# Two sets of weight buffers instead of three, with eight ring slots for row pairs and twelve for value rows

## The reference, cut to what matters

```python
def block(xb):                                    # 128 tokens; x is the normalised h
    q = einsum('td,de->te', xb, w_q)              # 8 heads x 2 halves x 128
    s = einsum('thpd,hpkd->thpk', q, keys)        # scores against 128 keys a half
    s_top, i_top = top_k(s, 16)
    cand = s_top[:, :, 0, :, None] + s_top[:, :, 1, None, :]
    best, sel = top_k(cand, 16)                   # 16 of 256 pairs of keys
    eidx = take_along_axis(cand_idx, sel)         # rows of 16384 experts
    gate = softmax(best)
    act = gelu(einsum('td,thkd->thk', xb, u_tab[eidx]))
    return einsum('thk,thkd->td', gate * act, v_tab[eidx])
y = rmsnorm(h + block(...), norm_final)
```

## Time and profile before

| | us |
|---|---|
| median of 3 runs | 2121.41 |
| lowest and highest | 2119.64, 2131.3 |
| profiled execution | 2125.79 |
| its span | 2123.7 |
| TensorE busy (matmul) | 1930.8, 91% |
| VectorE busy | 1360.7, 64% |
| ScalarE busy | 608.8, 29% |
| GpSimd busy | 634.1, 30% |
| first part of the stage | about 820 to 1503 |
| second part of the stage | about 1520 to 2116 |

### The profile page before, as it was taken

How to read it: one execution, slowest core, us unless ns; L and a number is a source line. 1 busy time by engine, 2 the same in 40 slices (tenths; PEclk the granted TensorE clock), 3 DMA queues, 4 the chain that set the end, 5 groups by cost and what they waited for, 6 DMA issues and landing times. The chain is left out here.

```text
span 2123.7 us, 29758 instructions
## 1 busy us (share of the span) xinstructions
PE 1930.8 (91%) x10912; PEld 1566.5 (74%) x10912; DVE 1360.7 (64%) x2860; ACT 608.8 (29%) x1217; POOL 634.1 (30%) x556
## 2 busy tenths in 40 slices
PE   5998889988996988989999999999899989999886
PEld 4997889977976988989999999989444333433332
DVE  3218274343346435479889888989677778776663
ACT  4223322252234424444444544444300000000000
POOL 0003021200000000312222222222477776776663
PEclk9999899998998999999999999999999999999999
DMA  3557158628614664799999999999899999999997
GB/s 114 195 198 228 34 165 268 224 75 268 214 59 146 227 234 145 289 341 385 374 369 391 379 383 363 370 363 378 314 412 411 395 410 411 398 400 415 408 412 289
DMA packets 230314, 629.25 MB, mean 296 GB/s; under 512 B 19714, under 2 KB 121157, under 8 KB 212376
## 3 DMA queue, kind: packets, MB, share of 16 engines
q0 software_dynamic: 74880, 377.52, 45.1%
q1 hardware_dynamic: 155296, 249.92, 34.5%
HBM read 584.36 MB, written 110.21 MB: 327 GB/s over the span
## 5 line engine op out<-in xcount | busy, mean ns | idle before, releaser
L2139 PE MATMUL ps<-ex_uv_row,ex_q_s 128*128 128x512 f32 (+1 forms) x1208 | 543.3, 601 | 62.4 <-DVE ex_q_s L2403 40.0
L2139 PEld LDWEIGHTS ps<-ex_uv_row,ex_q_s 128*128 128x128 f32 (+1 forms) x1208 | 217.3, 187 | 372.2 <-issue 355.8
L2068 POOL DMA_INDIRECT ex_uv_row<-value_rows,ex_eidx x384 | 404.5, 1053 | 187.5 <-issue 106.7
L589 PE MATMUL ps<-x_hi,ex_w_lo 128*128 128x384 f32 (+2 forms) x1296 | 426.3, 329 | 14.7 <-DVE ex_w_lo L1937 13.5
L590 PE MATMUL ps<-x_lo,ex_w_hi 128*128 128x384 f32 (+2 forms) x1296 | 424.4, 327 | 0.0
L591 PE MATMUL ps<-x_hi,ex_w_hi 128*128 128x384 f32 (+2 forms) x1296 | 424.2, 327 | 0.0
L2052 POOL DMA_INDIRECT ex_uv_row<-in_peer_uv,ex_eidx x128 | 147.3, 1151 | 470.3 <-DVE ex_fin L2390 464.7
L2390 DVE SCALAR_TENSOR_TENSOR ex_fin<-ex_uv_row,ret_tables,ex_fin 128x1024 f32<-128x1024 f32 x218 | 278.9, 1280 | 0.3
L589 PEld LDWEIGHTS ps<-x_hi,ex_w_lo 128*128 128x128 f32 x1296 | 245.1, 189 | 16.3 <-DVE ex_w_lo L1937 14.8
L591 PEld LDWEIGHTS ps<-x_hi,ex_w_hi 128*128 128x128 f32 x1296 | 245.5, 189 | 0.0
L590 PEld LDWEIGHTS ps<-x_lo,ex_w_hi 128*128 128x128 f32 x1296 | 245.3, 189 | 0.0
(11 more groups left out here) (415 smaller groups left out, 3417.7 us busy)
## 6 DMA issues: line engine op xcount, KB each, us to landing
value_rows<-in_peer_uv SPq DMA_DIRECT2D x64, 1024.0 KB
ex_w_raw<-in_peer_ut SPq DMA_DIRECT2D x128, 512.0 KB
value_rows<-ex_z_rows SPq DMA_DIRECT2D x128, 128.0 KB
first_raw<-in_w_in SPq DMA_DIRECT2D x8, 1024.0 KB, 7.6
ex_w_raw<-in_peer_wqt SPq DMA_DIRECT2D x16, 512.0 KB
value_rows<-ex_z_rows SPq DMA_DIRECT2D x128, 64.0 KB
dp_w_raw<-in_w_in SPq DMA_DIRECT2D x14, 512.0 KB
ex_uv_row<-value_rows,ex_eidx POOLq DMA_INDIRECT x384
```

Of the source, the lines that this page charges most:

```text
L589: pe.matmul(out, left(llo, c), right(rhi, c), start=(c == 0), stop=False)
L2068: pool.indirect_dma_start(value_slot(p)[0], None, k.value_rows, bass.IndirectOffsetOnAxis(ap=eidx[:, u, n % TOPK:n % TOPK + 1], axis=0), e ...
L2139: ins = pe.matmul(k.pv[j % 2][0:r, c, :], spread[:, on_tensor[p] % SPREADS, 0:r], v[:, c * 512:(c + 1) * 512], start=first, stop=last)
```

## The change

`DEEP` goes from 3 to 2, `RING` from 7 to 8 and `VALUES` from 10 to 12. With two sets, SyncE loads block i+2 in step i where it loaded i+3, after the low part of block i. ScalarE rounds block i+1 where it rounded i+2, after the same event. VectorE lowers block i+1 where it lowered i+2. The load and the rounding of block 2 ahead of the loop go away, as they are now part of it, and so does GpSimd's low part of block 4, which VectorE takes. The final gain uses the other buffer. The ring's memory grows from 56 to 64 KB a partition. As 136 pairs divide by 8, the value slots now begin at its start, and twelve fit.

```diff
--- before.py
+++ after.py
@@ -67,13 +67,13 @@
 HK = PH * TOPK
 NE = NK * NK
 PER_ROW = HK * NS // P
-RING = 7
-DEEP = 3
+RING = 8
+DEEP = 2
 AHEAD = 5
 BT = NP_TOK - P
 WROW = D + BT
 VALUE_SLOT = D + 2 * P
-VALUES = 10
+VALUES = 12
 ROWS_FROM = 6
 SPREADS = 6
 PARTS_AT = (1, 4, 7, 10)
@@ -1874,7 +1874,7 @@
         shift, tot = sb("shift", [P, UNITS + 1]), sb("tot", [P, UNITS + 1])
         eidx = sb("eidx", [P, UNITS + 1, TOPK], U32)
         eidx_s, gate_s = sb("eidx_s", [P, PER_ROW], U32), sb("gate_s", [P, PER_ROW])
-        x_rep, gain = sb("x_rep", [P, D])[:, :], w_raw[1][:, :, :].rearrange("p c n -> p (c n)")
+        x_rep, gain = sb("x_rep", [P, D])[:, :], w_raw[0][:, :, :].rearrange("p c n -> p (c n)")
         coef = k.ret[:, 0:SLOTS]
         fin, ms, unused = sb("fin", [P, 2, D]), sb("ms", [P, NT]), sb("unused", [P, 1])
         x_rest = flat(q)[:, 4 * D:8 * D].rearrange("p (t d) -> p t d", d=D)
@@ -1913,7 +1913,7 @@
 
         def by_dve(i):
 
-            return i not in (2, 3, 4)
+            return i not in (2, 3)
 
         def lowered(eng, i):
 
@@ -1994,7 +1994,6 @@
                 load(1)
                 for dst, src in h_out:
                     sp.dma_start(dst, src).then_inc(h_stored, 16)
-                load(2)
                 sp.wait_ge(h_stored, 32)
                 fetch(0)
                 fetch(1)
@@ -2069,7 +2068,7 @@
                                             bass.IndirectOffsetOnAxis(ap=eidx[:, u, n % TOPK:n % TOPK + 1], axis=0),
                                             element_offset=0 if n // HK == 1 else P).then_inc(value_loaded[b], 16)
 
-                for i in (2, 3, 4):
+                for i in (2, 3):
                     lower(pool, i)
                 for p in range(AHEAD):
                     gather_pair(p)
@@ -2275,7 +2274,6 @@
                 act.activation(q[:, 0:2, 0:P], k.pb[4][:, 0:2 * P].rearrange("p (n t) -> p n t", n=2),
                                ACT.Copy).then_inc(first_taken, 1)
                 upper_x(2)
-                upper(2)
                 upper_x(3)
                 upper_x(4)
                 act.wait_ge(cleared, 1)
@@ -2285,8 +2283,8 @@
                     elif i:
                         take(blocks[i - 1][1], 0)
                         take(blocks[i - 1][1], 1)
-                    if i and i + 2 < len(blocks):
-                        upper(i + 2)
+                    if i and i + 1 < len(blocks):
+                        upper(i + 1)
                     if row_at.get(i, 0) > 0:
                         row(row_at[i] - 1)
                     if i in weight_at:
@@ -2468,8 +2466,8 @@
                 retrieve(0)
                 for i in range(len(blocks)):
                     p = row_at.get(i, -1)
-                    if 5 <= i + 2 < len(blocks) and by_dve(i + 2):
-                        lower(dve, i + 2)
+                    if 4 <= i + 1 < len(blocks):
+                        lower(dve, i + 1)
                     if p >= 0:
                         dot(p)
                     if 1 < p <= HK + 1:
```

## The result

The changed kernel takes 2177.14 us (median of 4 runs, 2170.81 to 2180.03) beside 2126.36 for the kernel before (4 runs on the same chip, 2119.64 to 2132.22): a ratio of 1.022, 95% interval 1.0189 to 1.0251, so 2.2% slower. The forecast was 2183. Its mechanism, the turn of a weight buffer, is in the trace. How the sum came to 62 us holds less well, and that is what most experiments are about.

What follows compares the result with a forecast made beforehand. TensorE and the DMA engines were both taken as full beside the blocks, the DMA engines as binding the value part. Terms 25 + 30 + 6 + 8 - 2 - 5 = +62 us gave 2188, as a median 2183; range 2124 to 2262.

Steps and rivals of the forecast that it cites:

- The turn of a load: Experts' weight blocks: with two sets a buffer's turn, load to low part, exceeds two blocks' time; 0.2 us a block, +25 us.
- L: Time from a weight load's issue to its landing: 9.1 us read before, 6.5 assumed after; two sets hide 6.1.
- The retrieval on VectorE: Top-k parts beside the blocks make VectorE late with low parts and following loads: 0.75 us for each of 40, +30 us.
- The start: Opening of the experts stage: block 2's load waits for block 0's low part, amid eight gathers: +6 us (0 to +14).
- SyncE's lists: Two lists of small transfers issued between weight loads; with one set less, more of each delay is seen: +8 us.
- The ring slot: An eighth slot for pair gathers helps only in the last pairs, which have no blocks beside them: -2 us.
- The value slots: Twelve slots in the value part bring its DMA rate nearer its best slices: -5 us (-17 to 0).
- A: Two weight sets are enough, load time falling below 6.1 us: 2128 us, chance 0.13.
- B: Faster: no load late, lists and first burst hidden, value part at 412 GB/s: 2099 us, chance 0.10.
- C: The queue stays, load time remaining 9.1 us whatever the pace: +192 us on the blocks, 2320 us, chance 0.08.
- D: TensorE's pauses also drop its granted clock, once in each of nine units: +31 us on the forecast, 2214, chance 0.10.
- the marks set down: Signs expected in the trace: 16-block window, GB/s, TensorE's wait for low parts, load time, value part's length, clock mean.

Runs made afterwards that it cites:

- e7_a_dot: The changed kernel with the dots over 128 of 1024 columns, which relieves VectorE: 2173.59 us, ratio 1.0191.
- e4_b_raw2: The kernel before with only the loaded weights (w_raw) cut to two buffers: 2162.12 us, ratio 1.014.
- e1_raw3: The changed kernel with a third buffer for the loaded weights (w_raw) only: 2149.87 us, ratio 1.0086.
- e2_z3: The changed kernel with a third z_rows buffer only: 2176.9 us, ratio 1.0213.
- e3_raw3z3: The changed kernel with three w_raw and three z_rows buffers, two sets of rounded and low parts: 2130.39 us, ratio 1.0001.
- e10_r7v10: The changed kernel with seven ring slots and ten value slots: 2174.07 us, ratio 1.0211.
- e9_c_dot: e3_raw3z3 with the dots over 128 of 1024 columns: 2118.5 us, ratio 0.9962.
- e5_a_half: The changed kernel with pair gathers of half the size (only u, which stands in for v): 2121.42 us, ratio 0.9956.
- e6_b_half: The kernel before with pair gathers of half the size (only u, which stands in for v): 2103.44 us, ratio 0.9856.

## Why the prediction was right, and where its sum was not

**The turn of a load: the mechanism right, the size too low.** The prediction took L = 6.5 us between 4.0 and 9.1; measured 6.6 in the mean. That it came so near is luck: it was the middle of two values, and the 9.1 was read from two loads where the mean of the kernel before is 8.1. The load goes out ahead of the gather by 2.6 us (2.4 forecast), and half-size gathers lower L to 4.8, so it is shown that the gathers beside it make it long. Which of the two reasons that were given for a shorter L did it, the order or the slower pace, wasn't separated.

In the kernel before the turn wasn't what paced the loads, as SyncE's waits show, so that its 10.3 us of room with three sets is no limit there: one load in ten took over 10.3 us, and TensorE waited twice in the 110 blocks.

But (L + 2.31) / 2 with L = 6.5 gave 0.2 us a block and +25. The 110 blocks lost 42.8 us, 0.39 each. One mean L was put into a formula in which the loads over the limit count most; the early ones give nothing back beyond two sets. In the kernel after 75 of the 110 loads are above 6.1 us, by 90 us in all, and half of that, as a turn spans two blocks, is 45. That it comes so close is not to be relied on: in e7_a_dot the same sum gives 59 us, and its blocks lost 43.5. By the experiments the loads' third buffer is worth 30 us where all else has three (e4_b_raw2), 28 where z_rows stays at two (e1_raw3 against after), and 45 where z_rows has three (e2_z3 against e3_raw3z3: 0.0212 x 2127), of which 27 are in the 110 blocks and 7.5 in the opening, where block 2 is loaded earlier again.

The Trainium skill ("DMA: Bandwidth & Descriptors", on the anatomy of one DMA) would have a 512 KB load at an estimated 3.2 us; the page gives its figures for a transfer that GpSimd issues, and these loads are SyncE's. Not even the changed kernel, at 346 GB/s, comes near: 6.6 us. With gathers of half the size it is 4.8.

**The retrieval on VectorE: the addition failed.** It was to add 30 us to the turn. The waits that it named are there, 17.8 us in the 110 blocks, but e7_a_dot shows that relieving VectorE gives nothing back that can be told (ratio 1.0191 against 1.022; 30 us would be 1.4%), since the waits for loads grow by as much. In e3_raw3z3, where loads and stores hold up almost nothing, the lateness is worth 12 us against the kernel before in the 110 blocks. It lies beside the load's lateness, and the prediction added the two as if they followed each other. That VectorE's lateness gives the DMA engines time to catch up, which the prediction names, holds for the load too, and should have been carried through to the sum.

**The stores of z: a step that is missing.** z_rows is sized by the same constant. Its turn was never worked out, though it is the same sum: a store waits in the same queues, and ScalarE's activation waits for it. In the changed kernel it costs nothing by itself (e2_z3), with the loads cured 18 us (e1_raw3 to e3_raw3z3). For the total it makes no difference, for the question which buffer to give back it does.

Of +62 forecast and +50.8 measured, then, the first two terms (+55) stand for the blocks behind the opening, which lost 46.1 (42.8 and 3.3). If all of it is put down to the load's turn, as e7_a_dot suggests, one term is too small by 21 and the other too large by 30. The forecast came near in part because these errors have opposite signs, and that is luck too.

**The start** was to cost 6 us: the opening stretch lost 5.3, and TensorE has a wait of 5.3 us in it, at 887.0, that the kernel before has not. **SyncE's lists** were to cost 8, both together: nothing of it is seen. TensorE's waits behind them were 7.4 and 5.1 us before (at 924.0 and 1429.3) and are 4.0 and 3.6 after (at 928.9 and 1475.7), with one of 2.0 at 1463.5 while the second list is issued. **The ring slot** was to give 2 us: the hand-over is 5.5 us shorter, but most of that is there with seven slots too (e10_r7v10), and in e3_raw3z3 (14.7), whose blocks aren't late. It goes with having two rounded sets; by which of their effects wasn't settled. The slot itself is 1 us at most, and no run's time shows it. **The value slots** were to give 5 us: nothing that can be told, 2.5 to 3.6 us earlier gathers of which 2.5 are given back behind the last one. The DMA engines move 400 GB/s at a share of 1.00 with twelve slots as with ten.

**The rivals.** A (two sets are enough) and B (faster) fall by TensorE's idle time in every unit. C (L stays at 9.1) falls by L = 6.6; with three buffers and blocks that are hardly late it stays near the 8.1 of the kernel before (7.4 in e3_raw3z3, 8.0 in e9_c_dot). D (the clock falls too) didn't come: 1.00 granted in the mean of the 538.5 us. Of the marks set down, the unit (76 to 79 us: 77.5), L (5.8 to 7.3: 6.6), the value part and the clock are as forecast; its GB/s is 338 where 340 to 355 were named, TensorE's wait 52.0 us where 60 were, and its waits are 1.2 us in the mean but reach 5.3. "Most of them behind a retrieval part" is half right, 18 of 32.

## What to carry to other kernels

Where a constant counts buffers, list every pool that it sizes, the outgoing ones too, and work out each one's turn (issue, landing under load, what is computed on it) against the number of blocks that it may span; where two are short together, the longest lateness is seen and not their sum, so curing the shorter one alone shows nothing and curing the longer one alone only a part. Take a load's time from the loads of that very stretch, with its spread, since those over the limit cost most. Ask also which wait paces the loads now: a smaller ring can make another one the first. Here the large buffers of the turn were not equal: once loads and stores had three, the rounded and low parts could give up a set at no cost in the whole, while the loaded weights could not.

## What the runs showed of the hardware that was not expected

A load of 512 KB takes 4.8 us (mean) at a DMA share of 0.83 (e5_a_half, with half-size gathers), 6.6 at 0.96 (after) and 8.1 at 0.99 (before): its time rises most where the DMA engines are nearly full, so the time that a turn takes depends on its own pace (e6_b_half has 5.4 us at 0.82, so the share alone doesn't set it). Small transfers are no quicker: from the second issue of a z store (128 and 64 KB together) to its landing it is 6.7 us in the mean of the 110 blocks after the change, as long as a load of 512 KB, and 3.9 in e5_a_half. TensorE, stopped 32 times in these blocks for up to 3.6 us, has a mean granted clock of 1.00 (2.4 GHz), with 3.4 us at the lower level (1.2 GHz) behind the wait at 1475.7. In e7_a_dot it is stopped about as often, 26 times for up to 3.4 us, and the mean is 0.98, with five such stretches (near 993, 1051, 1143, 1395 and 1464); these 20 us have the longest (window, busy time by engine as above, granted clock 0.83):

```profile
1460.00:1480.00 20.00, 16.64 (x81) 16.32 (x80) 11.94 (x24) 7.02 (x15) 2.80 (x3) 0.83 0.93 334
```

Each of the five begins beside a wait of TensorE, of 2.6, 1.9, 2.5, 2.6 and 3.4 us. But a wait of 3.1 us in the kernel after, at 972.8, is followed by no lower stretch, so the length of the wait alone doesn't decide it; what does, the runs don't show. The Trainium skill ("TensorE: Matmul & The Clock Gate", on oscillation) warns of kernels whose matmuls wait for DMA in every tile. With TensorE busy for 502.9 of 538.5 us the trace of the kernel after shows one short fall; that of e7_a_dot agrees in kind, at a cost of 10 us.
